# A two-block model in fp32 split products: two more pairs of ff1 units by seven products, token sums made earlier, three low parts on POOL

## The reference

```python
def rmsnorm(x, g):
    xf = x.astype(jnp.float32)
    y = xf * lax.rsqrt(jnp.mean(xf * xf, axis=-1, keepdims=True) + RMS_EPS)
    return (y * g.astype(jnp.float32)).astype(x.dtype)

def sq_relu_mlp(h, w1, w2):
    return jnp.square(jax.nn.relu(h @ w1)) @ w2

h = h + m.astype(h.dtype)
h = h + sq_relu_mlp(rmsnorm(h, norm_mlp_g[i]), mlp_w1[i], mlp_w2[i]).astype(h.dtype)
...
f = jnp.square(jax.nn.relu(rms_norm(h, norm2_g[i]) @ w_ff1[i]))
h = h + f @ w_ff2[i]
```

## Time and profile before

| | us |
|---|---|
| median of 3 runs | 1307.53 |
| lowest and highest run | 1307.06, 1307.54 |
| the profiled execution | 1307.65 |
| its span, first to last instruction | 1305.9 |
| PE busy | 1283.7 (98%) |
| PE weight loads busy | 1085.8 (83%) |
| DVE busy | 957.8 (73%) |
| ACT busy | 690.4 (53%) |
| POOL busy | 16.5 (1%), 16 instructions |
| mean granted TensorE clock | 0.999 |

### The profile page before, as it was taken

How to read it: one execution, slowest core, us unless ns; L and a number is a source line. 1 busy time by engine, 2 the same in 40 slices (tenths; PEclk the granted TensorE clock), 3 DMA queues, 4 the chain that set the end, 5 groups by cost and what they waited for, 6 DMA issues and landing times.

```text
span 1305.9 us, 24372 instructions
## 1 busy us (share of the span) xinstructions
PE 1283.7 (98%) x9309; PEld 1085.8 (83%) x9309; DVE 957.8 (73%) x1543; ACT 690.4 (53%) x1100; POOL 16.5 (1%) x16
## 2 busy tenths in 40 slices
PE   6999999999999999999999999999999999999998
PEld 4788888888888998989887777788888989999876
DVE  7778778875767878777767777885777777776655
ACT  6766676765563434344446777733634444343452
POOL 0000000000000000000001000000000000000100
PEclk9999999999999999999999999999999999999999
DMA  4332222322234342333232222133243332322232
GB/s 162 79 92 63 77 77 69 81 66 82 72 107 132 96 125 91 105 96 98 65 98 81 65 65 71 59 97 113 83 159 97 98 96 96 98 96 88 75 95 97
DMA packets 40733, 119.52 MB, mean 92 GB/s; under 512 B 3984, under 2 KB 11600, under 8 KB 40656
## 3 DMA queue, kind: packets, MB, share of 16 engines
q1 hardware_dynamic: 33184, 114.78, 28.5%
q10 hardware_dynamic: 7472, 3.70, 1.7%
HBM read 116.34 MB, written 2.13 MB: 91 GB/s over the span
## 4 chain that ended last, share of the span: by engine, by line
PE 94%; DVE 3%; DMA 1%; ACT 1%; issue 1%; SPq 0%; ACTq 0%; DVEq 0%
PE acc L429 13%; PE acc L431 12%; PE acc L430 12%; PE ps L873 6%; PE ps L871 6%; PE ps L872 6%; PE acc L855 4%; PE acc L856 4%; PE acc L854 4%; PE ps L856 4%; PE ps L855 4%; PE ps L854 4%; PE ps L977 1%; PE ps L962 1%; PE ps L989 1%; DMA work<-rows 1%
## 5 line engine op out<-in xcount | busy, mean ns | idle before, releaser
L429 PE MATMUL acc<-xh,wh 128*128 128x512 f32 x624 | 259.2, 415 | 9.7 <-DVE xl L2598 8.8
L431 PE MATMUL acc<-xh,wl 128*128 128x512 f32 x624 | 244.6, 392 | 0.0
L430 PE MATMUL acc<-xl,wh 128*128 128x512 f32 x624 | 244.6, 392 | 0.0
L405 DVE TENSOR_TENSOR wl<-raw,wh 128x1024 fp32r<-128x1024 f32 x111 | 135.8, 1225 | 55.9 <-ACT wh L398 54.0
L429 PEld LDWEIGHTS acc<-xh,wh 128*128 128x128 f32 x624 | 117.9, 189 | 35.6 <-DVE wl L405 9.8
L431 PEld LDWEIGHTS acc<-xh,wl 128*128 128x128 f32 x624 | 117.6, 188 | 26.0
L430 PEld LDWEIGHTS acc<-xl,wh 128*128 128x128 f32 x624 | 118.0, 189 | 20.9 <-issue 1.2
L398 ACT ACTIVATE wh<-raw 128x1024 fp32r<-128x1024 f32 x111 | 115.8, 1049 | 29.7 <-DMA raw<-in_weights 20.3
L1495 ACT ACTIVATE wh<-raw 128x1024 fp32r<-128x1024 f32 x48 | 50.9, 1061 | 111.0 <-PE ps L856 111.0
L856 PE MATMUL acc<-yh,wl 128*128 128x512 f32 x256 | 99.9, 390 | 0.0
L855 PE MATMUL acc<-yl,wh 128*128 128x512 f32 x256 | 99.8, 390 | 0.0
(11 more groups left out here) (356 smaller groups left out, 2900.7 us busy)
## 6 DMA issues: line engine op xcount, KB each, us to landing
raw<-in_weights SPq DMA_DIRECT2D x208, 512.0 KB, 3.6
work<-rows ACTq DMA_DIRECT2D x14, 256.0 KB, 6.9
h<-in_xT SPq DMA_DIRECT2D x4, 512.0 KB, 6.6
outT<-h SPq DMA_DIRECT2D x8, 256.0 KB, 2.4
cst<-in_cst SPq DMA_DIRECT2D x1, 512.0 KB, 4.8
work<-in_pT SPq DMA_DIRECT2D x1, 512.0 KB, 4.6
kept<-in_keep SPq DMA_DIRECT2D x1, 208.0 KB, 6.2
work<-in_w_ab SPq DMA_DIRECT2D x1, 128.0 KB, 7.4
```

What stands on the lines that cost most here:

```text
L405: nc.vector.tensor_tensor(lo[:], raw[u.const % 2][:], hi[:].bitcast(F32), ALU.subtract).then_inc(lo_done, 1)
L429: nc.tensor.matmul(dst[:], hi, mh[:, k, :], start=(n == 0), stop=False)
L430: nc.tensor.matmul(dst[:], hi, ml[:, k, :], start=False, stop=False)
L431: mm = nc.tensor.matmul(dst[:], lo, mh[:, k, :], start=False, stop=(n == KT - 1))
```

## The change

The four plain ff1 units 4, 5, 8 and 9 of each feed-forward become two more pairs, so that the order of the 64 units is: four plain ff1 units, fourteen turns of a pair and two ff2 units, four ff2 units (the very last turn has one ff2 unit, as before). The order of the weights in memory stays. The remaining parts follow from that:

- X1 is copied by ACT beside the squares of the first four stream tiles (`act_norm_tile`), T1 and half of T2 are made by DVE ahead of the last stream tile (`dve_turned_first`), the rest in `dve_mlp`.
- The low parts of T1, T3 and T4 are made by POOL, which counts them in the new semaphore `turned_lo`; T2's stays on DVE. In the first pair PE waits for `turned_lo` ahead of its third and its fourth product.
- The pair waits at its start for the low part of its first unit alone, and for that of the second one ahead of its sixth product.
- In the first pair ACT copies the product m1 before the high parts of the ff2 weights (`act_first_product`).
- The first pair's weights are loaded through `load_half`, four buffers, from unit 4 on.

The diff, cut to its core (counts of semaphores that only follow from it are left out):

```diff
@@ load_mlp
-            load_units(sp, base, base + 12)
+            load_units(sp, base, base + 4)
             load_half(sp, base, 0, 1)
-            with sp.Fori(1, 12) as n:
+            with sp.Fori(1, 14) as n:
                 load_half(sp, base, n, 3)
@@ pe_pair
-            pe.wait_ge(lo_done, u.number(2))
+            first = p == 0
+            pe.wait_ge(lo_done, u.number(1))
...
             product(ps[1][:, lo_t], a_hi[0], a_lo[0], *x_of(0, lo_t))
+            if first:
+                pe.wait_ge(turned_lo, 3 * mlp_no(base) + 1)
             product(ps[3][:, lo_t], s_hi[0], s_lo[0], *t_of(0))
+            if first:
+                pe.wait_ge(turned_lo, 3 * mlp_no(base) + 3)
...
             product(ps[0][:, lo_t], a_hi[1], a_lo[1], *x_of(4, lo_t))
+            pe.wait_ge(lo_done, u.number(2))
@@ pe_mlp
-            for n in range(6):
+            for n in range(4):
                 ff1(n)
-            pe_ff2(pe, Unit(base + 6), 0, (hid_count(base), 0, 0))
-            pe_ff2(pe, Unit(base + 7), 0)
-            for n in range(8, 10):
-                ff1(n)
-            pe_ff2(pe, Unit(base + 10), 0)
-            pe_ff2(pe, Unit(base + 11), 0)
...
+            turn(base + 4, 0, 0, 2, False)
+            turn(base + 8, 0, 1, 3, False)
@@ block.gpsimd
+            for base in (U_FF1, U_FF2):
+                first = (2 if base == U_FF1 else 4) * KT
+                for n in (0, 2, 3):
+                    pool.wait_ge(sumh_d, H + 36 * mlp_no(base) + 4 + n + 1)
+                    if n == 0:
+                        pool.wait_ge(sum_d, H + 69 * mlp_no(base) + 5)
+                    nc.gpsimd.tensor_tensor(Tl[n], Tf[n], Th[n].bitcast(F32), ALU.subtract).then_inc(turned_lo, 1)
@@ act_norm_tile
+            if m < 4:
+                nc.scalar.activation(X1[:, m, :], h[:, m, :], ACT.Copy, scale=pc(gname, m)).then_inc(sumh_d, 1)
@@ act_mlp
+            split_hi(act, Unit(base + 2))
+            turned_hi(0)
+            act_rstd(act, 2 if base == U_FF1 else 3, ps[0][:], rstd, 1.0 / D)
+            split_hi(act, Unit(base + 3))
+            act_hidden(act, base, Unit(base), 0, 0, hr, hs)
+            for n in range(1, 4):
+                turned_hi(n)
+            act_hidden(act, base, Unit(base + 1), 1, 1, hr, hs)
+            act_first_hi(act, base, 0, 0, Unit(base + 4))
+            act_sums_hi(act, base, 0, 0)
...
@@ dve_mlp
+            dve_turned_rest(dve, base)
+            dve_relu(dve, base, 0)
+            split_lo(dve, Unit(base + 3))
+            dve_hidden_lo(dve, base, 0, 0, hs)
+            dve_turned_last(dve, base)
+            dve_relu(dve, base, 1)
+            dve.wait_ge(sumh_d, H + 36 * m + 6)
+            dve.wait_ge(sum_d, H + 69 * m + 13)
+            nc.vector.tensor_tensor(Tl[1], Tf[1], Th[1].bitcast(F32), ALU.subtract)
+            dve_sums(dve, base, 0, 0, first)
+            dve_last_sum(dve, base, 0, 0, first)
+            dve_hidden_lo(dve, base, 1, 1, hs)
+            dve_relu(dve, base, 2)
+            dve_sums_lo(dve, base, 0, 0)
+            dve_first_lo(dve, first)
...
@@ block.vector, the output projection before each feed-forward
+                if n == 6:
+                    dve_turned_first(dve, U_FF1)
             dve_stream_norm(dve, KT - 1, "mlp_g")
+            split_lo(dve, Unit(U_FF1 + 2))
```

More of the change, by code:

```diff
@@ L1527, in act_mlp @@
             m = mlp_no(base)
[L1528 to L1546, removed]
@@ L2185, in dve_ff2 @@
             nc.vector.tensor_tensor(h[:, 2 * q + 1, :], ps[4 + b][:], h[:, 2 * q + 1, :], ALU.add).then_inc(evac[b], 1)
-        def dve_turned(dve, base):
-            m = mlp_no(base)
[L2191 to L2214, removed]
-                    nc.vector.scalar_tensor_tensor(out=f[3][:, k, :], in0=h[:, 4 + k, lo_t], scalar=gain(4 + k),
-                                                   in1=f[1][:, k, :], op0=ALU.mult, op1=ALU.subtract).then_inc(sum_d, 1)
-            def low(n):
-                def step():
-                    dve.wait_ge(sumh_d, H + 32 * m + 4 + n + 1)
-                    nc.vector.tensor_tensor(Tl[n], f[n], Th[n].bitcast(F32), ALU.subtract)
-                return step
-            return [t1, t2, t3, t4] + [low(n) for n in range(4)]
@@ new lines, in turned_gain, with dve_turned_second, dve_turned_first @@
+        def turned_gain(base, k):
+            return pc("mlp_g" if base == U_FF1 else "n2_g", k)
+        def dve_turned_second(dve, base, tiles):
+            for k in tiles:
+                nc.vector.scalar_tensor_tensor(out=Tf[1][:, k, :], in0=h[:, 4 + k, hi_t], scalar=turned_gain(base, 4 + k),
+                                               in1=Tf[0][:, k, :], op0=ALU.mult, op1=ALU.subtract).then_inc(sum_d, 1)
+        def dve_turned_first(dve, base):
+            m = mlp_no(base)
+            dve.wait_ge(sumh_d, H + 36 * m + 4)
+            nc.vector.tensor_tensor(Tf[0], X1[:, :, hi_t], X1[:, :, lo_t], ALU.subtract).then_inc(sum_d, 1)
+            dve.wait_ge(sum_d, H + 69 * m + 1)
+            dve_turned_second(dve, base, range(2))
@@ L2321, in dve_mlp @@
             tile_n[0] += KT
-            t1, t2, t3, t4, l1, l2, l3, l4 = dve_turned(dve, base)
-            beside = ((), (t1, t2), (t3,), (t4,), (), (l1, l2))
-            for n in range(6):
-                split_lo(dve, Unit(base + n + 2))
-                dve_relu(dve, base, n)
-                for step in beside[n]:
-                    step()
-                dve_hidden_lo(dve, base, n, n, hs)
-            for n in range(6, 8):
-                split_lo(dve, Unit(base + n + 2))
-                (l3, l4)[n - 6]()
-                dve_ff2(dve, Unit(base + n), n - 6)
```

121 lines of the change are left out of this document (73 added, 48 removed).

## The result

| | us |
|---|---|
| before, median of 5 runs beside it | 1307.53 |
| changed kernel, median of 5 runs | 1314.17 |
| its lowest and highest run | 1312.69, 1315.34 |
| ratio, with its 95% interval | 1.0047, 1.0036 to 1.0058 |
| its profiled execution, span | 1314.62, 1312.8 |

The kernel became slower, by 0.5%. The forecast was 1311.8 us, slower by 0.3%; the median lies 0.17 us above the upper end of the range. Profiled execution against profiled execution it is +6.97 us, where the sum said +4.2.

What follows compares the result with a forecast made beforehand. The prediction took PE, busy 98% of the span, as the bound. Saving 3.3 us and adding stands of 3.35 and 4.15 us gave +4.2 us on the profiled 1307.65 us; it said 1311.8 us, range 1305 to 1314.

Steps and rivals of the forecast that it cites:

- What bounds, and where it breaks: PE bounds; it idles once, 3 to 4 us, before each feed-forward's first product, until DVE makes unit 4's low part.
- PE's saving, 3.3 us: Two ff1 units (10.88 us) become a seven-product pair (10.05 us): 0.83 us per pair, two pairs in each of two feed-forwards.
- the 4.8 us by 6 cycles plus columns: Alternative saving of the four pairs by the Trainium skill's matmul price at 2.4 GHz, not used in the sum.
- POOL's price, 2.4 us: Time taken for one POOL subtraction of 1024 columns, between bounds 1.29 and 2.97 us; it holds DVE 2.25 us.
- Blocks of 2.25, 1.65 and 2.25 us: DVE's holdups in the second feed-forward by POOL's low parts of the first, third and fourth token sums.
- the three instructions named: DVE work said to be held by POOL: third sum's tiles, low part of the second sum, first weight sum.
- the two meetings of the earlier trace: POOL and DVE overlapping at 685.05 and 1237.73 us, read as the two taking turns, whole instructions long.
- Slack: DVE's lead before the first pair without POOL: 1.75 us in the second feed-forward, 0.95 us in the first.
- -3.3 + 3.35 + 4.15 = +4.2 us: PE's saving from the pairs plus its stands in the second (3.35 us) and first (4.15 us) feed-forward.
- rival 1: POOL's parts cost DVE nothing that counts, so all 3.3 us stay: 1304.3 us, faster by 0.25%; chance 0.14.
- its condition: DVE's blocking by POOL stays under the slack of 1.75 and 0.95 us in the two feed-forwards.
- Rival 3: POOL slower still beside DVE, 2.97 us each, 3.4 us more in all: 1315.2 us; chance 0.08, inside the slow case.

Runs made afterwards that it cites:

- m1_first: dve_late with ACT copying m1 ahead of the fourth hidden tile in the first pair, not behind it: 1304.16 us, ratio 0.9976.
- dve_late: Changed kernel with the three low parts on DVE, right behind the low part of unit 4, none on POOL: 1304.57 us, ratio 0.9979.
- fill: Changed kernel with 14 unused matmuls of 128x512 on PE right ahead of the first pair of each feed-forward: 1311.42 us, ratio 1.0030.
- pool_memset: pool_scratch with POOL only writing, three fills of 2048 columns at the same places instead of the subtractions: 1304.84 us, ratio 0.9985.
- pool_first: dve_late with the low part of T1 on POOL, where the changed kernel has it: 1305.17 us, ratio 0.9980.
- pool_scratch: dve_late plus POOL's same three subtractions at the changed kernel's places, written to free space and unused: 1315.93 us, ratio 1.0065.
- dve_before_sums: dve_late with the three low parts on DVE ahead of the first weight sum: 1307.16 us, ratio 0.9999.
- no_lows: Changed kernel without POOL's six subtractions, products reading the high parts of T1, T3 and T4 instead, result not the model's: 1304.17 us, ratio 0.9978.

## Why the prediction was nearly right

- **What bounds, and where it breaks**: as forecast. One stand in each feed-forward, ended by unit 4's low part on DVE, no other wait new.
- **PE's saving, 3.3 us**: 3.45 in `m1_first` by the profiled executions (1307.65 - 1304.20). Right; the spacing in the trace was the price to take, the 4.8 us by 6 cycles plus columns were not there.
- **POOL's price, 2.4 us**: 2.52. Blocks of 2.25, 1.65 and 2.25 us: 2.15, 1.6 and 2.2, at the three instructions named, and turn about as the two meetings of the earlier trace rows had shown.
- **Slack**: 1.75 us in the second feed-forward, exactly. In the first I took 0.95, since unit 2's low part ends 0.8 us later there; it is 1.75 too (`dve_late`), because without POOL DVE has caught up and waits for PE at 370.28. That was wrong, and my own schedule had the time to catch up in, 0.56 us ahead of the first relu (911.9 to 912.46) and 0.28 ahead of unit 2's (921.8 to 922.08). In the changed kernel DVE catches up less: of blocks of 5.95 us, by the difference, 0.25 went into waits and 1.75 into slack, so PE stood 3.95 where 4.15 was forecast; in the second feed-forward 1.1 and 1.75, so 3.1 against 3.35.
- **The step that failed is the sum itself**: "-3.3 + 3.35 + 4.15 = +4.2 us" prices the stands at their own length. The terms in it came out at -3.3 + 3.1 + 3.95 = +3.75. Missing is a term for PE after the stand, two stretches at the lower clock, 1.5 us each in the profiled execution; `fill` puts it at 2.75 to 3.15 us. With 2.75 the sum would have been 1314.6; without it the measured median lies above the range. The trace before had a row for it that I did not read, the start of the program, where PE had stood 8.76 us:

```profile
8.76 0.76 PE L429 MATMUL acc<-xh,wh 128*128 128x512 f32 x1 [8.76 <-DVE xl L2598]
...
10.61 0.63 PE L430 MATMUL acc<-xl,wh 128*128 128x512 f32 x1
11.03 0.63 PE L431 MATMUL acc<-xh,wl 128*128 128x512 f32 x1
...
13.26 0.39 PE L431 MATMUL acc<-xh,wl 128*128 128x512 f32 x1
13.49 0.40 PE L429 MATMUL acc<-xh,wh 128*128 128x512 f32 x1
```

  The starts are 0.427 us apart at first, 0.23 later: some 4 us at the lower level after a stand, so about 2 us lost. A stand of 0.9 us has nothing of the kind behind it, nor has one of 1.9 us in the same trace (61.13, shown in the last section). Between 1.9 and 8.76 us this trace left it open, which is a bound on both sides that the range should have held: 0 to 2 us for each stand, and its upper end near 1316.
- **Rivals**: rival 1 (1304.3 us) is the time without POOL's reads, which `pool_memset` (1304.84) comes near; its condition, blocks that waits and slack take up, is what `pool_first` meets. Rival 3 had the total nearly right, 1315.2, by luck: its price of POOL (2.97) is refuted by the trace (2.52).

## What to carry to other kernels

On an engine that is busy all the time, price a new stand as its length plus what the clock costs behind it, and look for rows of the same trace that show PE after a stand; take that cost as a range, since the same stand had it in one execution and not in another. Before an operation goes to POOL to relieve DVE, ask what each of them reads: two SBUF operands on DVE against a reading POOL gives no second engine but one path used in turns, with POOL taking 2.52 us for what DVE does in 1.14. Often it is enough to make the thing later on the same engine, behind what the waiting engine needs first.

## What was not expected of the hardware

- After stands of 3.1 to 3.95 us, two each in `pool_scratch` and the changed kernel, the granted clock fell to the lower level (0.213 us between 256-column starts); after the two of `dve_before_sums`, 1.4 and 1.3 us, it did not. The fall came at once on restart in the second feed-forward and in `pool_scratch`, 1.16 us after it in the first of the changed kernel, and the stretch lasted from 3.15 to 5.9 us.
- The length of a stand alone does not decide it. Every kernel here, the one before too, has a stand of 1.9 us near 61 us, far ahead of the change. Behind it the starts of 512-column matmuls lie 0.23 us apart in five of the ten profiled executions (the kernel before, the changed one, `dve_late`, `fill`, `dve_before_sums`) and 0.427 in four (`no_lows`, `pool_scratch`, `pool_memset`, `m1_first`). In the tenth, `pool_first`, the fall comes behind a stand of 1.5 us at 73.26, where `dve_late` has one of 1.4 and no fall. The kernel before, then `m1_first`:

```profile
61.13 0.44 PE L627 MATMUL ps<-work 32*32 32x16 f32 x32 [1.88 <-DVE work L1915]
...
62.12 0.39 PE L430 MATMUL acc<-xl,wh 128*128 128x512 f32 x1
62.35 0.39 PE L431 MATMUL acc<-xh,wl 128*128 128x512 f32 x1
```

```profile
60.69 0.44 PE L628 MATMUL ps<-work 32*32 32x16 f32 x32 [1.88 <-DVE work L1925]
...
62.63 0.63 PE L431 MATMUL acc<-xl,wh 128*128 128x512 f32 x1
63.05 0.63 PE L432 MATMUL acc<-xh,wl 128*128 128x512 f32 x1
```

  What decides between the two is open; no run here varied it.
- Whether the slow stretches make the time less steady is not shown. The five runs of the changed kernel lie 2.65 us apart and the five of the kernel before beside them 0.52, but the 27 runs of the kernel before beside `no_lows` lie 2.2 us apart (1306.47 to 1308.69).
- In the first 4 us of the kernel before in which PE works, the starts show the lower level while the granted clock is listed as 1.00; the starts are the safer reading there.
